# Pair rows by indirect transfer and VectorE transposes, in place of gather matmuls, in a two-block hybrid model with experts

## The reference

```python
def hier_moe(h, w_grp, b_grp, w_rtr, b_rtr, w1, w3, w2):
    t = h.reshape(-1, d)
    grp_prob = jax.nn.softmax((t @ w_grp).astype(F32) + b_grp, axis=-1)
    g_prob, g_sel = lax.top_k(grp_prob, 1)
    exp_logits = ((t @ w_rtr).astype(F32) + b_rtr).reshape(-1, N_GROUPS, EXP_PER_GROUP)
    in_grp = jnp.take_along_axis(exp_logits, g_sel[:, :, None], axis=1)[:, 0]
    e_prob, e_sel = lax.top_k(jax.nn.softmax(in_grp, axis=-1), TOP_K_IN_GROUP)
    gate = g_prob * e_prob / jnp.sum(e_prob, -1, keepdims=True)
    ...
    hid = jax.nn.silu(jnp.einsum('td,edf->tef', t, w1)) * jnp.einsum('td,edf->tef', t, w3)
    y = jnp.einsum('tef,efd->td', hid * combine[..., None].astype(hid.dtype), w2)
```

## Time and profile before

| | us |
|---|---|
| median of 3 runs | 1307.88 |
| lowest and highest run | 1305.73, 1312.74 |
| span of the profiled execution | 1303.9 |
| experts' stage, layer 0 (chain of waits) | 581.3 to 806 |
| experts' stage, layer 1 (chain of waits) | 1070.3 to 1291 |
| TensorE, VectorE, ScalarE busy | 1269.3, 559.9, 486.9 |

### The profile page before, as it was taken

One profiled execution on the slowest core, in us unless ns is written; L12 is line 12 of the kernel. 1 busy time (PEld: TensorE's weight loads), 2 busy tenths in 40 slices (PEclk: granted clock), 3 DMA queues, 4 the chain that ended last, 5 costly groups with the idle time before them and its releaser, 6 DMA issues.

```text
span 1303.9 us, 19404 instructions
## 1 busy us (share of the span) xinstructions
PE 1269.3 (97%) x7567; PEld 815.6 (63%) x7567; DVE 559.9 (43%) x1226; ACT 486.9 (37%) x1066; POOL 115.5 (9%) x167
## 2 busy tenths in 40 slices
PE   9999999999999999999999998999999999999996
PEld 7888588885787877454344443788877554444432
DVE  3335223262676584342232215678485342222224
ACT  3346343462753245212223323663235312223232
POOL 0000000000014321000000000004322000000000
PEclk9999999999999999979999999999999999999998
DMA  9753162332521124749999999231132859999994
GB/s 367 150 179 112 50 268 97 130 111 78 205 98 67 66 98 172 308 170 377 420 420 420 422 416 407 100 113 67 66 130 99 341 213 397 419 421 420 422 420 195
DMA packets 48848, 307.40 MB, mean 236 GB/s; under 512 B 5897, under 2 KB 6409, under 8 KB 16752
## 3 DMA queue, kind: packets, MB, share of 16 engines
q1 hardware_dynamic: 43760, 288.61, 56.0%
q0 software_dynamic: 3200, 8.16, 2.8%
q10 hardware_dynamic: 1792, 9.31, 1.9%
HBM read 301.05 MB, written 8.59 MB: 237 GB/s over the span
## 4 chain that ended last, share of the span: by engine, by line
PE 80%; DVE 13%; ACT 5%; issue 2%; DMA 1%; ACTq 0%; DVEq 0%; SPq 0%
PE ps L1150 22%; PE ps L1840 18%; PE ps L1867 9%; PE ps L1417 4%; PE ps L1190 4%; PE ps L1909 2%; PE ps L1930 2%; PE ps L1118 2%; DVE projT L2792 1%; DVE small L2791 1%; PE ps L1158 1%; PE ps L1649 1%; PE ps L1849 1%; DVE projT L2783 1%; PE ps L1540 1%
## 5 line engine op out<-in xcount | busy, mean ns | idle before, releaser
L1150 PE MATMUL ps<-hT,ring 128*128 128x272 f32 (+1 forms) x1760 | 416.8, 390 | 0.6 <-ACT hT L2027 0.6
L1150 PEld LDWEIGHTS ps<-hT,ring 128*128 128x128 f32 x1760 | 327.1, 190 | 62.6 <-issue 7.0
L1840 PE MATMUL ps<-ring,arena 128*64 128x512 f32 x416 | 139.4, 600 | 0.0
L3157 DVE TENSOR_TENSOR xo<-ps,xo 128x512 fp32r<-128x512 f32 x64 | 42.9, 689 | 99.3 <-ACT xo L2465 99.3
L3278 POOL TENSOR_TENSOR arena<-projT,cst 32x272 f32<-32x272 f32 x104 | 71.6, 689 | 114.1 <-DVE projT L2770 101.0
L1840 PE MATMUL ps<-projT,arena 128*64 128x512 f32 x240 | 80.0, 597 | 0.0
L3148 DVE TENSOR_TENSOR arena<-arena,ps 128x256 f32<-128x256 f32 x32 | 13.5, 422 | 140.0 <-ACT arena L2452 139.4
L1840 PEld LDWEIGHTS ps<-ring,arena 128*64 128x64 f32 x416 | 40.1, 137 | 52.0 <-issue 51.2
L2450 ACT ACTIVATE arena<-ps 128x256 f32<-128x256 f32 x32 | 12.3, 386 | 138.7 <-PE ps L1840 138.7
L1417 PE MATMUL ps<-ring,projT 128*128 128x512 f32 x128 | 56.6, 596 | 0.0
L1190 PE MATMUL ps<-ring,arena 128*128 128x512 f32 x128 | 55.9, 593 | 0.0
(11 more groups left out here) (518 smaller groups left out, 2045.8 us busy)
## 6 DMA issues: line engine op xcount, KB each, us to landing
ring<-experts SPq DMA_DIRECT2D x72, 1024.0 KB, 16.2
ring<-w_in SPq DMA_DIRECT2D x62, 1024.0 KB, 5.4
projT<-experts SPq DMA_DIRECT2D x48, 1024.0 KB, 15.6
arena<-experts SPq DMA_DIRECT2D x22, 1024.0 KB, 12.8
prm<-experts SPq DMA_DIRECT2D x22, 1024.0 KB, 15.9
ring<-w_out SPq DMA_DIRECT2D x16, 1024.0 KB, 4.8
spare<-experts SPq DMA_DIRECT2D x12, 1024.0 KB, 14.5
lent<-experts SPq DMA_DIRECT2D x8, 1024.0 KB, 10.1
```

Of the source, the lines that this page charges most:

```text
L1150: mm = pe.matmul(ps[:, chunk_bank(blk, l, j), 0:ncols], w[:, j % 2, k, :], hT[:, k, T - ncols:T], start=(k == 0), stop=(k == KC - 1))
L1840: mm = pe.matmul(ps[64 * e:64 * e + 64, 0, :], xg[:, 4 * h + k, i % 2, 64 * e:64 * e + 64], w[e][:, k // 2, 512 * (k % 2):512 * (k % 2) + ...
L3157: v.tensor_tensor(low, ps[:, 4 + half, :], high, ALU.subtract).then_inc(s("pair_rows_copied"), 1)
```

## The change

Group 0 stays as it was. Pairs 4 to 15, those of groups 1 to 3, no longer pass through `gather_two` and `tokens_in`. In their place GpSimd fetches each pair's 128 slots on their own (`turned_pairs`, 12 indirect transfers a layer where there were 3), into one of three buffers, and `turn_tokens` on VectorE turns them into `xg` by 16 transposes of 32 partitions by 256 elements. The token of each slot comes out of `gate_slots` as a 17th column (`slot_tokens`). So that the indices are known early, a group's work (`turn_group`, `select_pairs`, `gates_in`, `gate_slots`) moves ahead by two steps, that of group 1 into step 0, and `psel` gets a second buffer. `xselT` and this buffer lie in `hT`, so that `lent` serves all 96 loads.

```diff
@@ -42,7 +42,7 @@
 CONSTS_ROOM, NORMS_ROOM = 15, 16
 ALL_SLOTS = 17
 
-LAST_USE = {LENT: 57, ONCE[1]: 75, CONSTS_ROOM: 79, NORMS_ROOM: 79}
+LAST_USE = {ONCE[1]: 75, CONSTS_ROOM: 79, NORMS_ROOM: 79}
 SLOT = 2048
...
@@ -628,6 +630,20 @@
 
             return 16 + 16 * (l + 1) + 16 * min(l + 1, LAYERS - 1)
 
+        def turned_pairs():
+
+            return range(PAIRS_A_GROUP, PAIRS)
+
+        def fetched_by(l, i=None):
+
+
+            return 16 * ((PAIRS - PAIRS_A_GROUP + 1) * l + (1 if i is None else i - PAIRS_A_GROUP + 2))
...
         xrows, ax = more(ax, D)
-        xplaces, ax = more(ax, 3 * PER_GROUP)
-        psel = halved("psel", ax, PER_GROUP, EXPERT_SLOTS)[:, :, :]
+        xplaces, ax = more(ax, 4 * PER_GROUP)
+        psels = [halved("psel", ax, PER_GROUP, EXPERT_SLOTS)[:, :, :],
+                 nc.alloc_sbuf_tensor_at("psel_odd", [P, PER_GROUP, EXPERT_SLOTS], F32R, offset=hT_at + 4 * D)[:, :, :]]
+        xselT = hT.rearrange("p k n -> p (k n)")[:, D + PER_GROUP * EXPERT_SLOTS:D + PER_GROUP * EXPERT_SLOTS + T]
...
@@ -849,7 +868,9 @@
         xo = halved("xo", ax, 2, D)[:, :, :]
         ax += 2 * D
 
+        pair_rows = [xrows, whole(rows_low), whole(rows_high)]
         slot_gates = small[:, 132:140].rearrange("p (b q) -> p b q", b=2)
+        slot_tokens = ctx.enter_context(nc.sbuf_tensor("slot_tokens", [P, 2, PAIRS_A_GROUP], I32))[:, :, :]
...
                     w = [expert_in(pe, ("up", l, i, h, e)) for e in range(2)]
-                    pe.wait_ge(s("pair_tokens_copied"), copies_of(i) - (h == 0))
+                    if i < PAIRS_A_GROUP:
+                        pe.wait_ge(s("pair_tokens_copied"), copies_of(i) - (h == 0))
+                    else:
+                        pe.wait_ge(s("row_places"), places_left(i))
                     if h == 0 and i:
...
@@ -1855,13 +1880,14 @@
                     pe.wait_ge(s("pair_hidden_copied"), i + 1)
                     if i:
                         pe.wait_ge(s("pair_rows_copied"), 2 * i)
-                    if i % PAIRS_A_GROUP == 1 and i + PAIRS_A_GROUP < PAIRS:
-                        gate_slots(i // PAIRS_A_GROUP + 1)
-                    if i == PAIRS_A_GROUP * (GROUPS - 2) + 1:
+                    before = i % PAIRS_A_GROUP == PAIRS_A_GROUP - 1 and i + 1 < PAIRS_A_GROUP * (GROUPS - 1)
+                    if before:
+                        gate_slots(i // PAIRS_A_GROUP + 2)
...
@@ -1947,18 +1973,19 @@
                             add_up(i - 2)
                         if q == 1:
                             turn_pairs(g)
-                        if q == 2 and g + 1 < GROUPS:
+                        if q == 0 and g + 1 < GROUPS:
                             turn_group(g + 1)
                         up_half(i, 1)
-                        if i % 2 and i + 1 < PAIRS:
-                            gather_two(i + 1, 0)
+                        if i == 1:
+                            gather_two(2, 0)
                         if i:
                             down(i - 1)
                         if i == 0:
                             gate_slots(0)
                             gather_pair(1)
-                        elif i % 2 and i + 1 < PAIRS:
-                            gather_two(i + 1, 1)
+                            gate_slots(1)
+                        if i == 1:
+                            gather_two(2, 1)
 
 
...
@@ -2481,12 +2508,12 @@
                             g, q = i // PAIRS_A_GROUP, i % PAIRS_A_GROUP
                             if i:
                                 hidden_in(i - 1)
-                            if q == 2 and g + 2 == GROUPS:
+                            if q == 0 and g + 2 == GROUPS:
                                 turned_in()
                             if q == 1 and g:
                                 sums_in(g - 1)
                             gate_sigmoid(i)
-                            if i == 0 or i % 2 and i + 1 < PAIRS:
+                            if i < 2:
                                 tokens_in(i + 1)
...
@@ -3104,36 +3136,51 @@
                         chosen(2, PER_GROUP).then_inc(s("pairs_selected"), 1)
                         return
                     v.wait_ge(s("group_places_in"), g + 2)
-                    VP(v.tensor_copy(xplaces, ps[:, 5, 0:3 * PER_GROUP]))
+                    VP(v.tensor_copy(xplaces[:, 0:3 * PER_GROUP], ps[:, 5, 0:3 * PER_GROUP]))
+                    VP(v.tensor_reduce(xplaces[:, 3 * PER_GROUP:3 * PER_GROUP + 1], xplaces[:, 2 * PER_GROUP:3 * PER_GROUP], AX, ALU.add))
                     chosen(0, PER_GROUP).then_inc(s("pairs_selected"), 1)
...
                         .then_inc(s("pairs_selected"), 1)
 
                 def gates_in(g):
 
 
                     v.wait_ge(s("pair_gates_done"), g + 1)
+                    if g:
+                        facts = ps[:, 5, 32:32 + SLOT_FACTS * PAIRS_A_GROUP].rearrange("p (q n) -> p q n", n=SLOT_FACTS)
+                        VP(v.tensor_scalar(slot_tokens[:, g % 2, :], facts[:, :, SLOT_FACTS - 1], -0.5, float(NO_ROW - T // 2),
+                                           ALU.mult, ALU.add))
...
-
...
-                        v.wait_ge(s("pair_gathered"), 4)
...
-                    v.tensor_tensor(rows_low, xrows, rows_high, ALU.subtract).then_inc(s("rows_split"), 1)
+                    v.tensor_tensor(rows_low, xrows, rows_high, ALU.subtract).then_inc(s("row_places"), 1)
+
+                def turn_tokens(i):
+
+                    v.wait_ge(rows_fetched, fetched_by(l, i))
+                    v.wait_ge(up_used, 2 * PAIRS * l + 2 * (i - 2) + 2)
+                    rows = pair_rows[(i - PAIRS_A_GROUP) % 3].rearrange("p (k j r) -> p k j r", j=4, r=32)
+                    for j in range(4):
+                        for slots in range(4):
+                            here = slice(32 * slots, 32 * slots + 32)
+                            ins = v.transpose(xg[32 * j:32 * j + 32, :, i % 2, here], rows[here, :, j, :])
+                    ins.then_inc(s("row_places"), 1)
 
                 def pairs_in(g):
...
                             pairs_in(g)
-                        if q == 2 and g + 1 < GROUPS:
+                        if q == 0 and g + 1 < GROUPS:
                             select_pairs(g + 1)
                             gates_in(g + 1)
-                        if q == 3 and g + 1 < GROUPS:
-                            split_rows(g + 1)
+                        if i == 2:
+                            v.wait_ge(s("pair_gathered"), 6)
+                            v.sem_inc(s("row_places"), 2)
                         hidden(i)
                         if i == 0:
-                            split_rows(0)
+                            split_rows()
                         if i:
                             rows_out(i - 1)
-                        if q == 2 and g + 2 < GROUPS:
+                        if q == 0 and g + 2 < GROUPS:
                             select(g + 2)
+                        if i + 2 in turned_pairs():
+                            turn_tokens(i + 2)
                     chosen_added(VP)
...
@@ -3296,17 +3347,25 @@
                       s("pool_product_ready"))
                 if l < LAYERS - 1:
                     clear(mixer_over, LAYERS + l + 1, names + names_2, mixer_go)
-                for group in range(GROUPS):
-                    g.wait_ge(s("group_tokens_ready"), group + 1)
-                    if group == 0:
-                        g.wait_ge(rows_stored, 16 * (3 * l + len(tiles_of(l))))
-                    if GROUPS * l + group:
-                        g.wait_ge(rows_fetched, 16 * (GROUPS * l + group))
-                    g.indirect_dma_start(xrows, None, normed_rows,
-                                         bass.IndirectOffsetOnAxis(ap=group_tokens[:, group:group + 1], axis=0),
+                g.wait_ge(s("group_tokens_ready"), 1)
+                g.wait_ge(rows_stored, 16 * (3 * l + len(tiles_of(l))))
+                if l:
+                    g.wait_ge(rows_fetched, fetched_by(l - 1, PAIRS - 1))
+                g.indirect_dma_start(xrows, None, normed_rows,
+                                     bass.IndirectOffsetOnAxis(ap=group_tokens[:, 0:1], axis=0),
+                                     bounds_check=T - 1, oob_is_err=False).then_inc(rows_fetched, 16)
+                for i in turned_pairs():
+
+                    group, q = i // PAIRS_A_GROUP, i % PAIRS_A_GROUP
+                    g.wait_ge(s("pair_gates_copied"), group + 1)
+                    g.wait_ge(s("row_places"), 1 if i == PAIRS_A_GROUP else max(3, places_left(i - 3)))
+                    g.wait_ge(rows_fetched, fetched_by(l, i - 1 if i > PAIRS_A_GROUP else None))
+                    g.indirect_dma_start(pair_rows[(i - PAIRS_A_GROUP) % 3], None, normed_rows,
+                                         bass.IndirectOffsetOnAxis(ap=slot_tokens[:, group % 2, q:q + 1], axis=0),
                                          bounds_check=T - 1, oob_is_err=False).then_inc(rows_fetched, 16)
```

(35 more changed lines are left out.)

40 lines of the change are left out of this document (22 added, 18 removed).

## The result

| | us |
|---|---|
| before, median of 4 runs on this chip | 1308.93 (1305.73 to 1312.74) |
| after, median of 4 runs | 1327.19 (1324.97 to 1328.21) |
| ratio after to before | 1.0151, 95% interval 1.0134 to 1.0167 |
| span of the profiled execution | 1326.0 (before 1303.9) |

The change makes the kernel slower by 1.5%. The ratio gives 19.8 us (17.5 to 21.8), the two spans 22.1 us. The forecast was 1323 us, 15.0 us more than before, with a range of 1312 to 1336. All ratios here leave out three single executions among the experiments that were far slower than the others of their kernel (1939, 2130 and 7186 us).

The account below looks back on a forecast made before the run. The prediction took the weights' bytes to bound each stage's end, with TensorE a close second. Row fetches of 5.8 us plus a later start of 9.2 us, added to 1307.9 us, gave 1323 us, range 1312 to 1336.

Parts of the forecast that it names:

- The bound: At the end of each expert stage the weights' bytes arrive last, at 421 GB/s; TensorE is a close second.
- The rival in which TensorE was the bound: TensorE sets the end of the stages, so the changed kernel is faster: 1288 us; chance 0.06.
- The signs named in the forecast: Included TensorE waits of 5 to 15 us in each stage's last four pairs and SP's issue 5 us later.
- The later start: Step 0 of each layer: work put ahead of `up_half(1, 0)` delays the next loads, 5.0 + 4.2 us.
- a rival of 18 us a pair: TensorE idles at the stage's end and its clock falls to 1.2 GHz: 18 us for one pair, 1341 us; chance 0.03.
- The row bytes: Rows of groups 1 to 3 fetched twice, in more transfers, none of it hidden: 5.8 us for both layers.
- The sum: Row fetches plus later start, nothing gained from TensorE: 5.8 + 9.2 - 0 = 15.0 us more; chance 0.74.
- what was put at zero: TensorE's saved products, `lent`, VectorE's transposes and waits such as transposes ahead of `select_pairs`: 0 us in the sum.
- The free price: VectorE's 16 transposes a pair fit beside its other work: no cost up to about 0.6 us a transpose.
- the rival decides: VectorE becomes the bound from about 0.8 us a transpose: 1342 us at 0.9, 1469 us at 1.23; chance 0.04.
- `lent` and the gather products: One more place for loads and six fewer `gather_two` calls a stage on TensorE: both put at zero gain.

Follow-up runs that it names:

- the two edits: Changed kernel with pairs 4 to 15 fetching no rows and group 1's selection moved to step 1: 1305.05 us, ratio 0.9979 to before.
- The filled waits: Changed kernel with unused matmuls in TensorE's two waits of step 0: 1320.43 us, ratio 1.0097 to before.
- the run without row bytes: Changed kernel with all slot indices of the pair fetches out of bounds, so no rows come in: 1317.09 us, ratio 1.0063 to before.
- the run with the second copy aside: Kernel before, rows of groups 1 to 3 fetched a second time into a room nobody reads: 1314.27 us, ratio 1.0047 to before.

## Why the prediction was right, and where its sizes were off

**The bound.** Right. Three things show it: 29.1 us of products removed from the kernel before gave nothing, 1.78 MB of rows that nobody reads cost 6.1 us, and the two edits add up. The rival in which TensorE was the bound (1288 us) falls with the first of these. The signs named in the forecast came true in kind. The waits for weights begin before the last four pairs, at 727 us in layer 0, and SP's issue behind `up_half(1, 0)` comes 8.5 us later in that stage, not 5.

**The later start.** Forecast 5.0 + 4.2 = 9.2 us, seen in the chains of waits 8.5 + 6.0 = 14.5 us. Without the slowed up halves (5.28 - 3.58, and 5.35 - 3.65 in each layer, 5.1 us) it is 5.1 + 4.3 = 9.4 us. So the forecast's instructions and waits were counted right. What was missing from this term is the lower clock of the products behind the waits. The filled waits show it for the second wait of each layer, by 3.4 us in the chain and 7.1 us in the time. Taking the late start away gave 11.1 us, some 3 us less than the chain's 14.5. The line of loads may absorb that much; the difference is also about the size of the uncertainty. That 11.1 lies so near to 9.2 is therefore partly luck: 5.1 us were not counted, and some 3 us of the chain did not reach the time.

**The clock.** I had looked for this at the end of the stage, as a rival of 18 us a pair, and put nothing down for it at the start. At the end it did happen (`up_half` at 776.29 us took 5.35 us after a wait of 2.59), but only now and then: other products there took 3.65 us after waits of 0.98 to 2.19 us. And there TensorE waits for weights anyway. The Trainium skill's page "TensorE: Matmul & The Clock Gate" (section "HAM oscillation — how this bites in real kernels") describes products that start at the lower clock after each wait for data. The trace agrees at the start of the stages for three up halves of four, with 1.7 us each, and only partly at the end.

**The row bytes.** Forecast 5.8 us, of it 4.0 for 1.78 MB and 1.8 for 18 more transfers. Measured for the bytes: 5.7 us, half of the 11.5 us that 3.57 MB cost, or 6.1 us with six of the transfers. The price per MB was too low by the run without row bytes, 2.25 us where it gives 3.2 (2.5 to 4.0). The interval of the run with the second copy aside (3.9 to 8.5) holds the forecast's 4.6. I had taken the price from the queue's own packet time, and that itself was right: 5.9 us more than before by the page (3.2% of 1326.0 less 2.8% of 1303.9), against 5.8. What the packet time leaves out isn't found in the weights' packets, whose time is the same with and without the rows, and stays open.

**The sum.** 11.1 for the start and 5.7 for the bytes make 16.8 of the 19.8 us. The 3.0 us left would be the transfers without rows (1.8 us by the forecast's price) and what was put at zero. No run has measured these alone, and with 2.9 us of uncertainty the rest may be nothing.

**VectorE.** The transposes are free, as forecast, at 435 ns where 0.42 us was taken from an operation on the same 256 columns. No run left them out; that four more cost nothing, and that start and bytes make up all but 3.0 us, is what shows it. The Trainium skill's page "VectorE: DVE Perf Modes" (section "The three transpose paths") has 311 ns for a transpose of 128x128 in bf16; the trace's float32 transpose of 32x256 takes 1.4 times that. The free price "up to about 0.6 us" also stands: 20 transposes are as much as 16 of 0.54 us, and 24 as much as 16 of 0.65 us. Wrong was the point from which the rival decides, "about 0.8 us a transpose". I had counted 2.2 us of other work a pair. That holds for a plain pair (2.3), but a group's first two pairs carry its selection too. From 640 to 720 us VectorE is busy for 64.25 of 80 us, and a pair takes 12.6 us on average (`hidden` at 649.86 and, six pairs later, 725.22), so it works 10.1 us a pair, 7.0 of them transposes and 3.1 other. With 24 transposes this makes 10.4 + 3.1 = 13.5 us. That leaves nearly nothing of the 13.7 us that a pair of the stage could take on average before, and with the waits between the engines a pair took 14.7 us (`hidden` at 638.32 and, eleven pairs later, 800.54).

**`lent` and the gather products.** Worth nothing, as forecast; both were run.

## What to carry to other kernels

When two engines look full, look at the end of the stage and ask which arrives last, then take work from one of them: products worth 29 us were free here, and 1.78 MB of rows were not. Before moving selection work ahead of a bound stage, count the waits it puts in front of the first products, and allow for a slowed product behind each (three of four were slowed here). A test of "more bytes" must put them where no engine waits for their landing.

## What the runs showed of the hardware

- At the start of layer 0's stage, the 16 products behind a wait of 1.0 us took 5.28 us in place of 3.58. In layer 1, behind a wait of 0.9 us, they took 3.58. The granted clock had been 0.50 from 576 to 582 us ahead of the first, and 1.00 from 1060 us on ahead of the second; no run tests whether that tells them apart. Later waits of 0.98 to 2.19 us had no such effect either, one of 2.59 us had it.
- One filler product of 384 columns ahead of the first wait did not keep the clock up in layer 0 (0.73 granted over the 5 us behind it); two of 448 columns ahead of the second wait did, in both layers (3.65 us in place of 5.35).
- Transfers by indirect index cost 3.2 us of time per MB (2.5 to 4.0), and 2.3 us of their own packet time, beside a full queue of weights, while the weights themselves move at 2.4 us per MB (421 GB/s).
- A VectorE transpose of 32 partitions by 256 float32 elements takes 435 ns, 421 to 442 over all 384, about as long as an elementwise operation on as many columns (421 ns, L3195).
